# Nine more places for gathered expert rows, and h read from PSUM by the last 256 dots

## The reference, cut to what matters

```python
q = (hf @ wq).reshape(t, PEER_HEADS, 2, PEER_DKEY // 2)
scores = jnp.einsum('thpd,hpnd->thpn', q, keys)
top_s, top_i = lax.top_k(scores, PEER_TOPK)
...
best_s, best_pos = lax.top_k(cand, PEER_TOPK)            # 16 experts for each token and head
expert = jnp.take_along_axis(cand_idx, best_pos, axis=-1)
gate = jax.nn.softmax(best_s, axis=-1)
def block(args):                                         # 128 tokens, 8 * 16 experts each
    u = jnp.take(u_tab, e_blk, axis=0)
    act = jax.nn.gelu(jnp.einsum('td,tkd->tk', h_blk, u)) * g_blk
    vv = jnp.take(v_tab, e_blk, axis=0)
    return jnp.einsum('tk,tkd->td', act, vv)
h = _layernorm(DEEPNORM_ALPHA * h + _peer(h, ...), ln2_g, ln2_b)
```

## Time and profile before

| | |
|---|---|
| median of three runs | 3764.18 us (3756.61 to 3775.44) |
| span of the profiled execution | 3894.7 us |
| own time of the profiled execution beside its span | not recorded |
| PE, DVE, ACT, POOL busy | 65%, 58%, 14%, 59% of the span |
| software DMA queue (the gathers) | 1073.87 MB, 73.3% of 16 engines' span |
| all DMA | 1290.19 MB, mean 331 GB/s |
| granted clock of TensorE | mean 0.783 |

### The profile page before, as it was taken

One profiled execution on the slowest core, in us unless ns is written; L12 is line 12 of the kernel. 1 busy time (PEld: TensorE's weight loads), 2 busy tenths in 40 slices (PEclk: granted clock), 3 DMA queues, 4 the chain that ended last, 5 costly groups with the idle time before them and its releaser, 6 DMA issues.

```text
span 3894.7 us, 36528 instructions
## 1 busy us (share of the span) xinstructions
PE 2520.7 (65%) x11992; PEld 1555.7 (40%) x11992; DVE 2256.9 (58%) x5313; ACT 532.8 (14%) x1223; POOL 2313.9 (59%) x2086
## 2 busy tenths in 40 slices
PE   8788884557967876666977866557887700232354
PEld 6575763423735544434644534333644300000011
DVE  5243888854468776654468776555356678544300
ACT  3220321111003202211003202111000000000000
POOL 1000334776555667777556766677665677777765
PEclk9898996666988988768988988767898855565567
DMA  5223686899999999999999999999999999999998
GB/s 175 77 68 147 252 286 227 269 358 362 416 374 338 393 409 353 323 374 373 414 360 355 403 410 340 302 359 357 393 399 385 384 351 348 354 365 361 364 364 311
DMA packets 367620, 1290.19 MB, mean 331 GB/s; under 512 B 39468, under 2 KB 68148, under 8 KB 362308
## 3 DMA queue, kind: packets, MB, share of 16 engines
q0 software_dynamic: 294912, 1073.87, 73.3%
q1 hardware_dynamic: 66760, 201.39, 14.2%
q10 hardware_dynamic: 5760, 12.59, 0.8%
HBM read 1274.72 MB, written 12.98 MB: 331 GB/s over the span
## 4 chain that ended last, share of the span: by engine, by line
PE 28%; POOL 20%; DVE 15%; issue 14%; DMA 10%; another core or an unknown queue 6%; DVEq 3%; ACT 2%; SPq 0%; ACTq 0%; POOLq 0%
PE banks L1331 11%; POOL ring L648 11%; POOL ring L660 10%; DMA ring<-in_ev,idxT 7%; PE banks L1320 6%; DVE ring L1007 6%; PE banks L1341 4%; PE banks L1596 2%; PE banks L1542 1%; PE banks L1522 1%; DMA ring<-in_eu,eidx 1%; PE banks L1336 1%; DVE arena L961 1%; DVE arena L959 1%
## 5 line engine op out<-in xcount | busy, mean ns | idle before, releaser
L648 POOL DMA_INDIRECT ring<-in_eu,eidx x1024 | 1179.7, 1152 | 1106.3 <-DVE eidx L1289 397.6
L1007 DVE CUSTOM_DVE_ANT_0 ring<-ring,h_cur 128x1024 f32<-128x1024 f32 x1024 | 1216.8, 1221 | 320.1 <-DMA ring<-in_eu,eidx 277.2
L660 POOL DMA_INDIRECT ring<-in_ev,idxT x1024 | 1122.4, 1096 | 453.4 <-issue 299.4
L1320 PE MATMUL banks<-ring,wide 128*32 128x512 f32 x4096 | 722.4, 833 | 654.4 <-DMA ring<-in_ev,idxT 562.9
L1331 PE MATMUL banks<-arena,wslot 128*128 128x256 f32 (+1 forms) x3248 | 758.7, 391 | 28.1 <-ACT arena L760 11.6
L1331 PEld LDWEIGHTS banks<-arena,wslot 128*128 128x128 f32 (+1 forms) x3248 | 626.5, 195 | 198.1 <-issue 102.1
L1320 PEld LDWEIGHTS banks<-ring,wide 128*32 128x32 f32 x4096 | 147.7, 135 | 1074.7 <-issue 1030.4
L1341 PE MATMUL banks<-arena 128*128 128x128 f32 x1408 | 240.0, 335 | 73.0 <-ACT arena L809 29.8
L1341 PEld LDWEIGHTS banks<-arena 128*128 128x128 f32 x1408 | 219.5, 243 | 103.6 <-issue 42.1
L1331 PE MATMUL banks<-ring,wslot 128*128 128x256 f32 (+1 forms) x656 | 152.1, 389 | 11.5 <-DMA wslot<-in_w_sm 7.2
L1336 PE MATMUL banks<-ident,arena 128*128 128x128 f32 x216 | 48.6, 379 | 161.4 <-DVE arena L978 52.7
(11 more groups left out here) (231 smaller groups left out, 2392.8 us busy)
## 6 DMA issues: line engine op xcount, KB each, us to landing
wslot<-in_w_pq SPq DMA_DIRECT2D x64, 576.0 KB
wslot<-in_w_mix SPq DMA_DIRECT2D x24, 1536.0 KB
wslot<-in_w_qkv SPq DMA_DIRECT2D x48, 512.0 KB
wslot<-in_w_fqk SPq DMA_DIRECT2D x32, 512.0 KB
wslot<-in_w_out SPq DMA_DIRECT2D x8, 2048.0 KB
ring<-in_eu,eidx POOLq DMA_INDIRECT x1024
ring<-in_ev,idxT POOLq DMA_INDIRECT x1024
wslot<-in_w_z SPq DMA_DIRECT2D x16, 512.0 KB
```

The lines of the kernel that those rows point to most:

```text
L648: pool.indirect_dma_start(out=ring[:, UPOS[k] % NR, :], out_offset=None, in_=eu, in_offset=bass.IndirectOffsetOnAxis(ap=eidx[:, n % (2 * T ...
L660: pool.indirect_dma_start(out=ring[:, VPOS[k] % NR, :], out_offset=None, in_=ev, in_offset=bass.IndirectOffsetOnAxis(ap=idxT[:, n % (2 * T ...
L1007: dve.tensor_tensor_reduce(out=row, in0=row, in1=h_cur[:, n % 3, :], scale=1.0, scalar=0.0, op0=ALU.mult, op1=ALU.add, accum_out=dots[:, n ...
L1320: last = pe.matmul(BY[k][32 * j:32 * j + 32, :], wide32[:, at:at + 32], ring[:, VPOS[4 * q + j] % NR, k * 512:(k + 1) * 512], start=(m == ...
```

## The change

1. **Places.** `slots()` gives each gather its place. Up to gather 1403 the places are those of before. At gather 1404 (`WIDE`; V token 636, the first that belongs behind `top 3 0`) nine places (`NX`) in columns 1024 to 10239 of `arena` are put ahead of the 15 in the rotation. From there on each place comes back after 24 gathers.
2. **A wait.** Gather 1404 waits until both tiles' transposes of the last block are in `h1T` (`s_hTe`) and until `h1` is stored (`s_h1st`).
3. **h from PSUM.** For tiles 6 and 7 ScalarE copies `h_cur` into banks 2 and 3 (tile 6) or 4 and 5 (tile 7), two copies of 128 x 512 each, and the dots of these tiles read h there in place of `h_cur`. The first dot of each waits for the copies (`s_hp`).

Nothing of the order of the gathers, dots or quads moves.

```diff
 NR = 15
+NX = 9
...
+def slots():
+
+    begin = UNITS.index(("top", NB - 1, 0)) + 1
+    at = UPOS + VPOS
+    wide = min([UPOS[k] for k in range(DOTS[begin], P * NT)] + [VPOS[k] for k in range(TOKS[begin], P * NT)])
+    turns, slot, turn, before = list(range(NR)), [], [], []
+    uses, held = {}, {}
+    for p in range(len(at)):
+        if p == wide:
+            turns = list(range(NR, NR + NX)) + turns
+        n = turns.pop(0)
+        turns.append(n)
+        uses[n] = uses.get(n, 0) + 1
+        slot.append(n)
+        turn.append(uses[n])
+        before.append(held.get(n))
+        held[n] = p
+    return slot, turn, before, wide
+
+SLOT, TURN, BEFORE, WIDE = slots()
+PLACED = UNITS.index(("idx", NB - 1, 0)) + 1
...
+        def place(p):
+
+            if SLOT[p] < NR:
+                return ring[:, SLOT[p], :]
+            return arena[:, D * (SLOT[p] - NR + 1):D * (SLOT[p] - NR + 2)]
+
+        hp = [banks[:, 1024 * (1 + k):1024 * (2 + k)] for k in range(2)]
...
             def place_free(p):
 
-                if p - NR in U_AT:
-                    pool.wait_ge(s_dot, U_AT[p - NR] + 1)
-                elif p - NR in V_AT:
-                    pool.wait_ge(s_vq, V_AT[p - NR] // 4 + 1)
+                if p == WIDE:
+                    pool.wait_ge(s_hTe, TT * NB)
+                    pool.wait_ge(s_h1st, 16 * NB)
+                if BEFORE[p] in U_AT:
+                    pool.wait_ge(s_dot, U_AT[BEFORE[p]] + 1)
+                elif BEFORE[p] in V_AT:
+                    pool.wait_ge(s_vq, V_AT[BEFORE[p]] // 4 + 1)
...
+                    if n >= NT - TT and s == max(FETCH[n], PLACED):
+
+                        act.wait_ge(s_h[n % 3], 16 * (n // 3 + 1))
+                        for k in range(2):
+                            last = act.activation(hp[n % 2][:, k * 512:(k + 1) * 512], h_cur[:, n % 3, k * 512:(k + 1) * 512], ACT.Copy)
+                        last.then_inc(s_hp, 1)
...
-                    dve.wait_ge(s_row[p % NR], 16 * (p // NR + 1))
-                    row = ring[:, p % NR, :]
+                    dve.wait_ge(s_row[SLOT[p]], 16 * TURN[p])
+                    row = place(p)
+                    if n >= NT - TT and c == 0:
+                        dve.wait_ge(s_hp, n - (NT - TT) + 1)
                     dve.tensor_tensor_reduce(
-                        out=row, in0=row, in1=h_cur[:, n % 3, :], scale=1.0, scalar=0.0,
+                        out=row, in0=row, in1=h_cur[:, n % 3, :] if n < NT - TT else hp[n % 2], scale=1.0, scalar=0.0,
```

More of the change, by code:

```diff
@@ L398, in build @@
         s_gx, s_gxe, s_sel, s_iT, s_ixT = (sem(n) for n in ("s_gx", "s_gxe", "s_sel", "s_iT", "s_ixT"))
-        s_row, s_dot, s_vq = sems("s_row", NR), sem("s_dot"), sem("s_vq")
-        s_gel, s_wm, s_wT, s_w32, s_yev = (sem(n) for n in ("s_gel", "s_wm", "s_wT", "s_w32", "s_yev"))
+        s_row, s_dot, s_vq = sems("s_row", NR + NX), sem("s_dot"), sem("s_vq")
+        s_hp, s_gel, s_wm, s_wT, s_w32, s_yev = (sem(n) for n in ("s_hp", "s_gel", "s_wm", "s_wT", "s_w32", "s_yev"))
         s_yv, s_ys, s_y, s_out, s_h = sem("s_yv"), sem("s_ys"), sem("s_y"), sems("s_out", 3), sems("s_hc", 3)
@@ L406, in flat @@
             return v.rearrange("p a b -> p (a b)")
+        def place(p):
[3 more added lines that the diff above has]
+        hp = [banks[:, 1024 * (1 + k):1024 * (2 + k)] for k in range(2)]
+        assert D * (NX + 1) <= after_rows
         def weights(name, n):
@@ L648, in gather_u @@
                 pool.indirect_dma_start(
-                    out=ring[:, UPOS[k] % NR, :], out_offset=None, in_=eu,
+                    out=place(UPOS[k]), out_offset=None, in_=eu,
                     in_offset=bass.IndirectOffsetOnAxis(
                         ap=eidx[:, n % (2 * TT), c // TOPK, c % TOPK:c % TOPK + 1], axis=0),
-                ).then_inc(s_row[UPOS[k] % NR], 16)
+                ).then_inc(s_row[SLOT[UPOS[k]]], 16)
             def gather_v(k):
@@ L660, in gather_v @@
                 pool.indirect_dma_start(
-                    out=ring[:, VPOS[k] % NR, :], out_offset=None, in_=ev,
+                    out=place(VPOS[k]), out_offset=None, in_=ev,
                     in_offset=bass.IndirectOffsetOnAxis(ap=idxT[:, n % (2 * TT), t:t + 1], axis=0),
-                ).then_inc(s_row[VPOS[k] % NR], 16)
+                ).then_inc(s_row[SLOT[VPOS[k]]], 16)
             for s in range(1, len(DOTS)):
@@ L1315, in experts @@
                         p = VPOS[4 * q + j]
-                        pe.wait_ge(s_row[p % NR], 16 * (p // NR + 1))
+                        pe.wait_ge(s_row[SLOT[p]], 16 * TURN[p])
                     for k in range(2):
@@ L1320, in experts @@
                             last = pe.matmul(BY[k][32 * j:32 * j + 32, :], wide32[:, at:at + 32],
-                                             ring[:, VPOS[4 * q + j] % NR, k * 512:(k + 1) * 512],
+                                             place(VPOS[4 * q + j])[:, k * 512:(k + 1) * 512],
                                              start=(m == 0), stop=(m == 31))
```

## The result

| | kernel before | changed kernel |
|---|---|---|
| median of the timed runs (4 each) | 3763.32 us (3756.61 to 3775.44) | 3732.16 us (3724.47 to 3734.59) |
| ratio, 95% interval | | 0.9897 (0.9875 to 0.9919) |
| profiled execution, span | 3894.7 us (first trace) | 3722.7 us |

The change makes the kernel faster by 31 us, or 1.0%. The forecast was 86. The two profiled executions differ by 172 us, which can't be the change: from the start of the program to the issue of gather 1400, where both kernels do the same, the changed one took 2845.9 us and the one before 2908.4. The first trace looks like one from a chip on which the whole kernel is slower than on the one that was timed (experiment e1 bears this out).

A forecast was written before the change was run, and what follows sets the result against it. It took the gathers as the bound, with GpSimd held back by VectorE's dots and waits for places. From gather 1404 on, 876 + 4 - 966 = -86 us, so 3764 - 86 = 3678 us, range 3652 to 3733.

The forecast's parts named there:

- 876 + 4 - 966: Gather 1404 to last data: 876 us at 400 GB/s plus 4 idle, against 966 traced, giving -86 us.
- changes of stage: Three stage changes, at tiles 5, 6 and 7, would leave some microseconds open, hence 400 GB/s instead of 411.
- If a dot with one operand in PSUM behaves as L1218 did: Dots of tiles 6 and 7 stop slowing gathers, like a half-width operation reading PSUM; 76 us of GpSimd's time go.
- They take away waits of 33 + 58 = 91 us: Nine more places end GpSimd's waits from gather 1404 on: 33 us for quads, 58 us for "remote".
- what it gains is inside the sum by bytes: The choice of experts ends on the gathers too; its gain is counted within 350.57 MB at 400 GB/s.
- I take 'remote' for the same thing: GpSimd's 58 us of waits the profile calls "remote" are waits for places, from late quad increments of `s_vq`.
- rival B: "Remote" waits aren't places and stay; only -60 to -65 us, 3702 us; chance 0.13.
- The wait at gather 1404: GpSimd stands 8 to 10 us for the store of `h1`; DMA engines run dry some 4 us, added as cost.
- Copies and dots: Tiles 6 and 7: ScalarE's four copies of h cost 0; dots every 1.15 to 1.28 us cost 0.
- rival D: Tile 6's stage: dots from PSUM at half rate, 2.2 us, make VectorE the bound; +114, 3792 us; chance 0.04.
- Rival A: Dots of tiles 6 and 7 go on disturbing gathers; only places pay, -45, 3719 us; chance 0.13.
- Rival C: 363 GB/s is the ceiling for gathers of 4 KB rows; nothing gained, 4 us lost, 3768 us; chance 0.09.

The follow-up runs named there:

- e1: Kernel before (3869.6 us) on a slow-kind chip beside nine places alone (1.0017), h from PSUM alone (0.997) and the change with places eleven gathers later (0.994).
- e4_before: Kernel before, unchanged, profiled on a chip of the kind the result was timed on: 3763.77 us, ratio 1.001.
- e1_before: Kernel before, unchanged, profiled a second time, on a slow-kind chip: 3873.62 us, ratio 1.0001.
- e3_after: The whole change, run again on a slow-kind chip against the kernel before (3899.36 us): 3872.28 us, ratio 0.9938.
- e1_psum: Kernel before plus h from PSUM only, 15 places, no wait at gather 1404, slow-kind chip: 3858.47 us, ratio 0.997.
- e3_narrow: The change with gathers of 896 instead of 1024 columns for tiles 6 and 7, slow-kind chip: 3875.72 us, 0.9947 of the kernel before.
- e2: On a second slow-kind chip, against the kernel before: the whole change 0.9972, nine places alone 1.002, h from PSUM alone 0.997.
- e3_few: The change with seven of eight matmuls of most quads of tiles 6 and 7 left out, slow-kind chip: 3859.28 us, 0.9898 of the kernel before.
- e1_places: Kernel before plus the nine places, without the PSUM operand, on a slow-kind chip: 3873.22 us, ratio 1.0017.

## Why the prediction was wrong

- **The start of the sum was wrong: "876 + 4 - 966", "profiled, 3894.7 becomes 3809", "I carry the microseconds over: 3764 - 86".** This step failed. The 966 us (363 GB/s) were those of a chip on which the kernel takes 3.5% longer; on the timed kind the same stretch takes 889 us at 394 GB/s (e4_before, 2853.45 to 3742.52). 77 of the 86 us were never there to be won. The text saw the 3.5% and took them for spread over the whole program. They weren't: 62 us lie before gather 1400, which is 2.2% of that part, and 77 in the stretch that the sum was about, 8.6%. The end of the sum was an absolute rate (400 GB/s) and the start a rate of the slower chip, so their difference counted the chip as well as the change.
- **The end of the sum was too long by 32 us.** 880 us were forecast, 848 measured (2861.20 to 3709.5), at 410 GB/s. The ceiling of 411 (853 us) was the right figure here, and "changes of stage" left nothing open. With both corrected, and 9 us since the stretch itself begins later by the wait in front of it: 86 - 77 + 32 - 9 = 32, against 31 in the medians and 32.7 in the spans (3755.4 to 3722.7). So the two errors partly cancelled, and the 31 us are no support for the 400 GB/s: from the true start, they would have given 9 us.
- **On the slow kind the start was right, and the forecast fails there too.** The stretch of the kernel before is 951 us in e1_before, near the 966 of the sum, but that of the changed kernel is 933 (e3_after, 373 GB/s), not 880: the "remote" waits stay, at 87 us. The change gained 12, 27 and 19 us there in the medians.
- **"If a dot with one operand in PSUM behaves as L1218 did": right.** Gathers of 936 to 948 ns in tile 6's stage of every kernel with it, on both kinds of chip, and 1.17 to 1.31 us in the mean beside dots from SBUF. The returned time was 43 us, not 76, since a gather beside dots from SBUF took less on the timed chip to begin with (1174 ns in tile 6's stage of e4_before), and nothing but tile 6's stage was short of it. Two lines of the earlier trace rows carried this over from an operation of half the width.
- **"They take away waits of 33 + 58 = 91 us": wrong on either kind.** On the timed chip there were 36, and 28 of them lay in the choice, where taking them away did not bring the first dot of tile 6 earlier. The sentence "what it gains is inside the sum by bytes" fell with it: the choice ended no sooner, and all that it left behind was seven or eight gathers more in hand.
- **"I take 'remote' for the same thing": wrong.** On the slow kind "remote" stays with 24 places (87 us in e3_after, of waits up to 5.9 us), as rival B said; on the timed kind it doesn't exist. B's price of 60 to 65 us came on neither kind. Where its start was right, the busy time that the dots gave back turned into more "remote" (60 to 97 us, e1_before to e1_psum). The wait shown in the earlier trace rows was read as a late quad, but nothing was weighed against the reading that this chip had a trouble of its own.
- **The wait at gather 1404**: 8.84 us long, as said. The DMA engines did run dry for some 4 us, as priced: in the changed kernel their busy share is 0.31, 0.00 and 0.52 in the three 2 us windows from 2858 on. Whether the kernel is longer for it can't be told: 0.9938 with it and 0.9923 without on the slow kind, and on the timed kind 863.6 against 866.7 us, the other way.
- **Copies and dots**: right. The copies cost 0 and a dot takes 1219 ns; rival D is out. (ScalarE's "4.1 us in 744" should read 4.28; nothing hangs on it.) Rival A is out, since the gathers take 940 ns beside the new dots. Its worry is real where the places stand alone on the slow kind (1314 ns against 1202).
- **Rival C** is out: 403 to 414 GB/s in every slice of e4_before's last stage but the one that holds the end. The rule of the Trainium skill ("SBUF — State Buffer") that was set beside it, 358 GB/s, is exceeded by that. The Trainium skill itself says elsewhere ("Perfetto Trace Analysis", the note under Roofline) that a core that is alone may take more than this share, up to about 435 GB/s of its 16 DMA engines. These traces agree: no slice shown here has more than 423.

What stays open is the cause of "remote" on the slow kind. Shown is that it isn't bytes (e3_narrow), that nine places more don't lessen it (e1, e2), and that with 24 places fewer matmuls do: in the last stage from 27 us to 13, of which 11.7 are one wait at the change of tile, and over the whole stretch from 87 us to 51 (e3_few). Few matmuls with 15 places, where the quads wait for rows and not for "issue", wasn't run. The profile of those chips records only 8 to 11 of the 16 increments of a gather's completion and gives no time to landing, so it doesn't tell which transfer is late. A theory is that one slow DMA engine holds back the last increment of each gather, until all places wait for it. No run tested it; an engine that is slower all the time doesn't go with e3_few, where such gathers flow at 408 to 422 GB/s for 120 us. A late last increment alone isn't enough either: in the last stage of the changed kernel on the timed kind it comes 5.1 us in the median behind the fifteenth (0.4 in e4_before), and the flow there has no dip.

## What to carry to other kernels

Before a sum is made against a traced stretch, hold the traced execution against the median of the timed runs: where they differ by more than the effect that is forecast, the trace shows a different machine or a different condition of it, and neither its microseconds nor its rates can be subtracted from another's. Say then for each wait whether it belongs to the kernel's own dependences (a quad, a dot) or only to something that the profile can't name ("remote"), and give the second kind its own case. Time given back to an issuing engine is worth only what the next consumer gets earlier, and can turn into another wait of the same engine (in e1_psum 63 us of it became 37 us of "remote" and 30 us of waiting for dots), so look for the operation that ends the stage first; and a VectorE operation that holds up gathers from GpSimd can be relieved by one operand in PSUM, at no cost in its own time.

## What the runs showed of the hardware

- The same program takes 3763 to 3767 us on some chips and 3869 to 3899 on others, at about the same granted clock (0.80, and 0.786 to 0.796). The slow kind shows periodic dips in the flow of gathers, from 412 or more to 240 to 340 GB/s in a slice of 4.5 us, with "remote" waits of GpSimd of 2 to 6 us, and its traces record 8 to 11 of the 16 increments of a gather's completion, where the others record all.
- A gather of 128 rows of 4 KB costs GpSimd 0.94 us alone or beside a 128 x 1024 VectorE operation with one operand in PSUM, and 1.17 to 1.31 us in the mean of a stage beside the same operation with both in SBUF. The Trainium skill ("SBUF — State Buffer", two separate sides) has a rule that fits: a VectorE operation with two SBUF inputs and a GpSimd operation that reads SBUF exclude each other at a shared pair of ports, for the whole of an instruction. The traces agree in that the time comes back when one input leaves SBUF; they don't show the ports.
- That VectorE operation takes 1218 to 1220 ns with an operand in PSUM, 1225 to 1229 with both in SBUF.
- One core moved 416 GB/s over 320 us and more (the third window of the changed kernel), with rows of 4 KB.
- More rows in hand can make the gathers beside VectorE's dots slower: on one chip 1314 and 1290 ns a gather with 24 places (e1_places), against 1202 with 15 (e1_before); on the timed kind 1211 and 1206 against 1174.
- On the slow kind TensorE stood 34 to 50 us for "issue" between its matmuls of the last stage with 24 places (44 in e3_after), and 0 to 13 us with 15 (7 in e1_before). On the timed kind it did so with neither.
